# Turning the hidden block of the expert waves by identity products in column tiles

## What is computed

```
def swiglu(x, w1, w3, w2):
    return (jax.nn.silu(x @ w1) * (x @ w3)) @ w2

for e in range(N_EXPERTS):
    out = out + gate[..., e:e + 1] * swiglu(x, w1[e], w3[e], w2[e])
```

## Time and profile before

| | |
|---|---|
| median of three runs | 2210.69 us (2207.57 to 2210.99) |
| the profiled execution | 2203.56 us |
| its span, first to last instruction | 2201.6 us |
| PE busy in the span | 2131.2 us (97%) |
| DVE busy | 746.1 us (34%) |
| ACT busy | 430.4 us (20%) |
| mean granted TensorE clock | 0.989 |

### The profile page before, as it was taken

How to read it: one execution, slowest core, us unless ns; L and a number is a source line. 1 busy time by engine, 2 the same in 40 slices (tenths; PEclk the granted TensorE clock), 3 DMA queues, 4 the chain that set the end, 5 groups by cost and what they waited for, 6 DMA issues and landing times.

```text
span 2201.6 us, 28675 instructions
## 1 busy us (share of the span) xinstructions
PE 2131.2 (97%) x12059; PEld 1227.1 (56%) x12059; DVE 746.1 (34%) x1529; ACT 430.4 (20%) x969; POOL 0.2 (0%) x4
## 2 busy tenths in 40 slices
PE   8988999999977999999999999999999999999998
PEld 5664777765754533333333323365677776667775
DVE  2563476323763100110110101035546743831112
ACT  2464000132463000000000001052410002420001
POOL 0000000000000000000000000000000000000000
PEclk9999999999989999999999999999999999999999
DMA  6222995233302999889999999723487651383230
GB/s 229 104 92 88 424 349 198 110 124 141 118 20 113 424 389 395 342 355 424 400 414 421 370 426 402 297 108 133 183 333 289 221 219 58 127 342 120 82 124 19
DMA packets 58340, 524.39 MB, mean 238 GB/s; under 512 B 8544, under 2 KB 9056, under 8 KB 20320
## 3 DMA queue, kind: packets, MB, share of 16 engines
q1 hardware_dynamic: 48992, 472.19, 53.1%
q10 hardware_dynamic: 9216, 50.34, 6.3%
HBM read 521.44 MB, written 1.06 MB: 237 GB/s over the span
## 4 chain that ended last, share of the span: by engine, by line
PE 88%; DVE 7%; ACT 3%; issue 1%; DMA 0%; DVEq 0%; ACTq 0%; SPq 0%
PE ps L90 88%; DVE ring L90 5%; ACT ring L90 2%; DVE stat L90 1%; ACT L90 1%; DVE natural L90 0%; DVE transposed L90 0%; DVE residual L90 0%; DVE gates L90 0%; ACT natural L90 0%; DVE z L90 0%; DMA residual<-in_x 0%; ACT z L90 0%; ACT transposed L90 0%; ACT gates L90 0%
## 5 line engine op out<-in xcount | busy, mean ns | idle before, releaser
L90 PE MATMUL ps<-ring 128*32 128x512 f32 (+10 forms) x3784 | 532.8, 517 | 15.7 <-ACT ring L90 6.3
L90 PE MATMUL ps<-ring,z 128*32 128x512 f32 (+3 forms) x2048 | 477.1, 586 | 2.1 <-ACT ring L90 1.2
L90 PE MATMUL ps<-ring,transposed 128*128 128x384 f32 (+4 forms) x1408 | 471.4, 491 | 3.1 <-DVE transposed L90 2.4
L90 PE MATMUL ps<-transposed,ring 128*128 128x257 f32 (+2 forms) x2128 | 470.2, 379 | 1.3 <-DVE transposed L90 1.3
L90 PEld LDWEIGHTS ps<-transposed,ring 128*128 128x128 f32 (+1 forms) x2128 | 399.8, 189 | 85.5 <-issue 30.4
L90 PEld LDWEIGHTS ps<-ring,transposed 128*128 128x128 f32 x1408 | 260.7, 191 | 186.5 <-issue 62.5
L90 PEld LDWEIGHTS ps<-ring 128*32 128x32 f32 (+4 forms) x3784 | 196.0, 129 | 297.6 <-issue 270.4
L90 PEld LDWEIGHTS ps<-ring,z 128*32 128x32 f32 (+2 forms) x2048 | 173.6, 140 | 250.8 <-issue 239.3
L90 DVE TENSOR_TENSOR z<-z,ps 128x256 f32<-128x256 f32 (+4 forms) x94 | 38.9, 414 | 547.1 <-ACT z L90 526.5
L90 ACT COPY z<-ps 128x256 f32<-128x256 f32 (+5 forms) x121 | 48.3, 399 | 511.9 <-PE ps L90 511.0
L90 ACT ACTIVATE z<-ps 128x256 f32<-128x256 f32 (+2 forms) x87 | 32.6, 374 | 443.2 <-PE ps L90 233.3
(11 more groups left out here) (138 smaller groups left out, 1029.6 us busy)
## 6 DMA issues: line engine op xcount, KB each, us to landing
ring<-in_moe SPq DMA_DIRECT2D x87, 2048.0 KB, 13.3
ring<-in_ffn SPq DMA_DIRECT2D x66, 1536.0 KB, 9.8
ring<-in_moe SPq DMA_DIRECT2D x90, 1024.0 KB, 12.0
ring<-in_w_in SPq DMA_DIRECT2D x25, 1536.0 KB, 6.4
z<-in_ada ACTq DMA_DIRECT2D x48, 768.0 KB, 5.3
ring<-in_w_out SPq DMA_DIRECT2D x12, 1536.0 KB, 7.4
natural<-in_ada ACTq DMA_DIRECT2D x16, 768.0 KB, 5.9
ring<-in_ple_gate SPq DMA_DIRECT2D x4, 1536.0 KB, 6.2
```

The lines of the kernel that those rows point to most:

```text
L90: self.ins = None if self.book.counting else op(*args, **kw)
```

## The change

The turn asks how wide the jobs of the turned wave are. For waves of the first expert (128 columns) nothing changes. For all others each block of 128 hidden units is turned by products with the identity: the block's columns are the stationary operand, 32 or 64 of them in each product, the identity is the moving operand, and the output goes to the same place in bank 6, 32 or 64 partitions in each product. The width is that of the turned wave, g - 1, whatever wave g, in the middle of which the turn stands, uses itself. Waits, signals and the copy by ACT stay.

```
+        wide = WAVES[g][2][0][1]
+        if wide == P:
+            for b in range(n):
+                pe(T.transpose, ps[:, 6, b * P:b * P + rows], mo_hid[0:rows, g % 2, b * P:(b + 1) * P], C("ident")[0:rows, 0:rows])
+            pe.then_inc(f"mo.turned{g}")
+            return
         for b in range(n):
-            pe(T.transpose, ps[:, 6, b * P:b * P + rows], mo_hid[0:rows, g % 2, b * P:(b + 1) * P], C("ident")[0:rows, 0:rows])
+            for at in range(0, P, wide):
+                mm(ps[at:at + wide, 6, b * P:b * P + rows], mo_hid[0:rows, g % 2, b * P + at:b * P + at + wide],
+                   C("ident")[0:rows, 0:rows])
         pe.then_inc(f"mo.turned{g}")
```

## The result

The kernel after takes 2214.54 us in the median against 2207.11 us for the kernel before in the same rounds, a ratio of 1.0032 with a 95% interval of 1.0020 to 1.0043: slower, by 4.4 to 9.5 us and 7.1 in the middle. The forecast was a loss of 6.4 us. The 2210.69 us from which the forecast started was the median of three runs, and it lies near the upper end of what eight runs showed.

What follows compares the result with a forecast made beforehand. PE was taken to bound the waves, with weight transfers following. Terms -1.5 + 2.8 + 1.9 + 0.4 + 2.8 = +6.4 us, put on the three-run median 2210.69, gave 2217.1 us; range 2211 to 2222.

Steps and rivals of the forecast that it cites:

- PE sets the pace: Waves, 740 to 1435 us: PE is busy for all 695 us, weight transfers follow, so longer PE work is paid.
- Products at 0.109 a group, 0.436 a turn: Changed turns: a block's identity products take two groups of 0.109 us, so a two-block turn takes 0.436.
- The rival that brought the loads into the open: Changed turns: every group of short products pays its weight load, 2222 us; chance 0.06.
- the one that made products cheap: Every changed turn: a block streams in one group instead of two, -11.0 us, giving 2206.1; chance 0.04.
- The bound for the loads in the open: Dearest product turn: 0.03 us on each of 4 groups in 47 turns and 2 in 7, +5 us, 2222.
- Matched turns, -1.5: 21 two-block turns with the surrounding wave's tiles, no side task behind: gain 0.07 us each, -1.5 us.
- 64-column turns in first-expert waves, +2.8: Five 64-column turns inside whole-array waves: new changes of tiling, loads and products lose 0.57 us each, +2.8 us.
- Mixed tiles, +1.9: Nine two-block turns, 32 in 64 or 64 in 32 columns, no side task: loss 0.21 us each, +1.9 us.
- One-block turns, +0.4: Six one-block turns without side task: two of 64 columns lose 0.11 us, four of 64 rows 0.05; +0.4 us.
- Side tasks behind, +2.8: 13 turns followed by a scatter, gather or gates task: losses of 0.07 to 0.42 us each, together +2.8 us.

Runs made afterwards that it cites:

- after, twice: Kernel after with every identity product of the 54 changed turns issued twice in the same place; stretch 745.76 us, 21.6 more than after.
- own tiles: Against the kernel after, turn width from the surrounding wave, transpositions kept in whole-array waves or before side tasks; 2202.15 us against 2206.47 before, ratio 0.9975.
- matched version: Against the kernel after, products only in 21 turns with the surrounding wave's tiles and no side task behind; 2204.69 us against 2207.22 before, ratio 0.9989.

## Why the prediction was right

The time came out 2.6 us under the forecast of 2217.1 and inside the range; the loss came out at 7.1 us by the ratio, which can't tell 4.4 from 9.5, and at 6.49 in the stretch, where 6.4 was forecast. So the mechanism was right, and its steps show it one by one. By these steps, from the distances between wave starts in both traces of after against before:

- *PE sets the pace.* Right on both sides: 6.5 and 28.1 us more work arrived in full (after, twice), and 3.6 us less were taken (own tiles). The transfers, at 0.94 of their engines, follow PE: SP's waits for it grew and shrank with PE's work.
- *Products at 0.109 a group, 0.436 a turn.* Right: 0.44 in the matched turn, 0.87 when doubled. The rival that brought the loads into the open, and the one that made products cheap, both fell here. (The bound for the loads in the open was added up wrongly: 0.03 on 202 groups is 6.1 us and not 5.)
- *Matched turns, -1.5.* -1.41: 0.07 or 0.08 in 17 of 21, 0.05 or 0.06 in the four in waves of two jobs. The fourth of these stands in the last wave; it is read from the matched version, where the last turn of all stayed a transposition.
- *64-column turns in first-expert waves, +2.8.* +2.78 by distances and by the experiment that undid them. The price of 0.22 before was read in the earlier trace rows from a turn of another kind, as said above; the right turn has the same.
- *Mixed tiles, +1.9.* +1.90: 0.22 in four (64 in 32), 0.21 in five (32 in 64).
- *One-block turns, +0.4.* +0.42: 0.11 in two, 0.04 in three, and 0.07 in the last turn of all (the last wave and this turn lost 0.02 together, of which the matched turn gained 0.05).
- *Side tasks behind, +2.8.* +2.80: the scatters 0.07 in six, 0.26 in the first expert's; 0.22 and 0.37 with gates; 0.40 to 0.42 with gathers. The one-block turn before a gather was the largest single miss, 0.31 for 0.26: the gather, from 910.43 to 914.07 before and from 921.01 to 924.75 after, grew by 0.10, the price of a product's first load in a new tiling. The prediction had this price for the gathers in its other items and took 0.05 here. Together these five items make +6.49.
- *The base.* I put the loss on a median of 2210.69 us from three runs. Eight runs gave 2207.11, 3.6 less. Between the medians of the eight runs of each kernel the loss is 7.4, 1.0 more than forecast. The two errors cancel in part: the time itself came out as near as 2.6 us by some luck, and only the stretch shows how near the sum was.
- *A bound with the wrong sign.* The prediction says that with a tenth less on every change of tiling the loss falls to about 5. By its own list the change removes 48 changes of tiling (two in each of 21 turns, one in each of 6) and adds 15, so a cheaper change of tiling raises the loss, to about 6.7. No run tested this, and the sum doesn't rest on it.

What the change meant to do, it did: in 21 turns both changes of tiling disappeared. It took the width from the turned wave, though. In 5 of the other turns that made changes of tiling where there were none; in others it left them, added a third or removed only one; and every changed turn paid double for its products. The own-tiles version keeps the idea and takes the width from the wave around the turn.

## What to carry to other kernels

A change of array tiling has a price that can be read off the starts in a timeline, here 0.10 us and a first load of 0.03 to 0.10; an operation is cheap in the tiling of its neighbours, so choose its form by what stands before and behind it in PE's queue and not by where its data came from. An identity product cost twice a transposition here, on 32-bit data, and paid only where it removed both changes of tiling around it. When a change is a fraction of a per cent, classify its instances by their neighbours and sum them; then compare the stretch that holds them in two traces: here it repeated to 0.01 us where the runs spread by several.

## What was not expected of the hardware

In the waves of two jobs only two of the four column tiles are at work. There the products of the turn, which come later in PE's program, began ahead of up products that come earlier. From the trace of after:

```profile
1050.50 1.68 PE L90 MATMUL ps<-ring 128*32 128x256 f32 x14
1051.81 0.41 PE L90 MATMUL ps<-constants,z 128*32 128x128 f32 x4
1052.01 0.39 PE L90 MATMUL ps<-ring 128*32 128x256 f32 x2
1052.23 0.61 PE L90 MATMUL ps<-constants,z 128*32 128x128 f32 x12
1052.66 1.68 PE L90 MATMUL ps<-ring 128*32 128x256 f32 x14
```

The half has sixteen up products; four turn products start at 1051.81, 0.2 us before the last two of them. The Trainium skill, page TensorE: Matmul & The Clock Gate, section Part 3: Packing small matmuls — row/col tiling, says that matmuls start and end in program order; here the starts don't. It gained nothing: the rest of the turn still takes 1052.66 - 1052.23 = 0.43 behind the last up products, as a whole matched turn does. The likely reason, argued from the kernel and not tested, is that the two busy tiles have their own share of the turn to do then.
